# A mixture-of-experts stage with 32-slot blocks in four column groups instead of 64-slot blocks in two

## The reference

```python
logits = (x @ router_w) + router_b
top_v, top_i = lax.top_k(logits, 4)            # 4 of 32 experts for each token
gates = jax.nn.softmax(top_v, axis=-1)
...
hdn = xblk @ w1[e] + b1[e]                     # 1024 -> 2048
g, up = hdn[:, :D_FF], hdn[:, D_FF:]
act = (clip(up, -7, 7) + 1.0) * (g * jax.nn.sigmoid(g * 1.702))      # g = minimum(g, 7)
y = act @ w2[e] + b2[e]                        # 1024 -> 1024
x = x + g2 * sum over the token's experts of gate * y
```

## Time and profile before

| | |
|---|---|
| median of 3 runs | 1650.99 us (1648.49 to 1652.93) |
| profiled execution, its time | 1649.28 us |
| profiled execution, its span (first to last instruction) | 1647.5 us |
| first W1 matmul of the expert loop | 648.89 us |
| TensorE busy | 1548.8 us (94%) |
| mean granted TensorE clock | 0.965 |

### The profile page before, as it was taken

How to read it: one execution, slowest core, us unless ns; L and a number is a source line. 1 busy time by engine, 2 the same in 40 slices (tenths; PEclk the granted TensorE clock), 3 DMA queues, 4 the chain that set the end, 5 groups by cost and what they waited for, 6 DMA issues and landing times.

```text
span 1647.5 us, 20298 instructions
## 1 busy us (share of the span) xinstructions
PE 1548.8 (94%) x8093; PEld 661.6 (40%) x8094; DVE 474.2 (29%) x791; ACT 318.8 (19%) x579; POOL 108.9 (7%) x111
## 2 busy tenths in 40 slices
PE   4989899978989898999999999999999999999996
PEld 4555555545544455333333333333333333333332
DVE  2141222147346254222222222222222222222224
ACT  1123332120231232111111111111111111111110
POOL 0000000120433250000000000000000000000000
PEclk8989998898998997999999999999999999999999
DMA  9462441341332650999999999999593999999993
GB/s 355 185 257 111 194 164 58 115 145 64 128 126 105 240 193 32 415 425 429 428 429 428 428 429 429 428 429 428 239 408 161 415 427 429 429 427 429 429 427 130
DMA packets 38583, 491.95 MB, mean 299 GB/s; under 512 B 4784, under 2 KB 4912, under 8 KB 9744
## 3 DMA queue, kind: packets, MB, share of 16 engines
q1 hardware_dynamic: 34144, 477.33, 70.1%
q0 software_dynamic: 4400, 14.06, 2.8%
HBM read 487.05 MB, written 4.33 MB: 298 GB/s over the span
## 4 chain that ended last, share of the span: by engine, by line
PE 89%; DVE 4%; DMA 3%; ACT 2%; issue 1%; POOL 1%; SPq 0%; DVEq 0%; POOLq 0%; ACTq 0%
PE ps L1609 28%; PE ps L1264 17%; PE ps L1638 15%; PE ps L1572 6%; PE ps L1558 6%; PE ps L1271 4%; PE ps L1200 4%; DMA ring<-in_w_dense 2%; PE ps L1223 1%; PE ps L1216 1%; PE ps L1614 1%; PE ps L1322 1%; PE ps L1342 1%; ACT ring L555 1%; PE ps L1520 1%
## 5 line engine op out<-in xcount | busy, mean ns | idle before, releaser
L1609 PE MATMUL ps<-ring,arena 128*64 128x512 f32 x2176 | 480.2, 594 | 2.9 <-issue 2.9
L1264 PE MATMUL ps<-ring,xT 128*128 128x512 f32 x672 | 306.2, 613 | 3.2 <-DMA ring<-in_w_dense 2.4
L1609 PEld LDWEIGHTS ps<-ring,arena 128*64 128x64 f32 x2176 | 156.7, 137 | 308.2 <-issue 305.6
L1638 PE MATMUL ps<-ring,arena 128*64 128x512 f32 x1088 | 248.5, 598 | 0.0
L1178 DVE TENSOR_TENSOR U<-ps,U 128x1024 f32<-128x1024 f32 (+1 forms) x102 | 124.4, 1220 | 248.9 <-PE ps L1572 248.9
L1264 PEld LDWEIGHTS ps<-ring,xT 128*128 128x128 f32 x672 | 129.2, 196 | 162.6 <-issue 158.2
L1638 PEld LDWEIGHTS ps<-ring,arena 128*64 128x64 f32 x1088 | 72.1, 136 | 168.1 <-issue 142.3
L1572 PE MATMUL ps<-arena 64*128 64x512 f32 x420 | 119.7, 636 | 0.8 <-ACT arena L741 0.8
L1558 PE MATMUL ps<-T,arena 128*64 128x512 f32 (+1 forms) x420 | 104.3, 615 | 1.2 <-DVE arena L1068 1.2
L714 ACT ACTIVATE W<-ps 128x512 f32<-128x512 f32 x35 | 20.9, 598 | 338.5 <-PE ps L1558 338.5
L1169 DVE TENSOR_SCALAR arena<-ps 128x512 f32<-128x512 f32 x34 | 23.5, 692 | 217.5 <-PE ps L1614 217.5
(11 more groups left out here) (261 smaller groups left out, 1043.7 us busy)
## 6 DMA issues: line engine op xcount, KB each, us to landing
ring<-in_w_moe SPq DMA_DIRECT2D x192, 2048.0 KB, 14.5
ring<-in_w_dense SPq DMA_DIRECT2D x33, 2048.0 KB, 8.6
V<-in_state POOLq DMA_DIRECT2D x6, 256.0 KB, 8.2
out_sample_retention<-V POOLq DMA_DIRECT2D x6, 256.0 KB, 2.8
R<-in_x_prompt SPq DMA_DIRECT2D x1, 1024.0 KB, 17.1
arena<-in_cache_kT POOLq DMA_DIRECT2D x8, 128.0 KB, 3.5
arena<-in_cache_v POOLq DMA_DIRECT2D x8, 128.0 KB, 3.6
arena<-in_b_gate POOLq DMA_DIRECT2D x4, 256.0 KB, 4.4
```

The source lines that it names most:

```text
L1264: last = mm(banks[t][0], xT[:, k, t * P:t * P + P], wv[:, k, :], start=(k == 0), stop=(k == KD - 1))
L1609: last = mm(ps[64 * a:64 * a + 64, half, :], xgT[:, k, j % 2, :], wv[:, k, HALF * a:HALF * a + HALF], start=(j % 2 == 0 and k == 0), stop= ...
L1638: last = mm(ps[64 * a:64 * a + 64, 2, :], actT[:, k, j - 4, :], wv[:, k, HALF * a:HALF * a + HALF], start=(j == 4 and k == 0), stop=(j == ...
```

## The change

- `BLOCK` is 32. With the counts above 8 experts need one block (0, 2, 5, 7, 25, 26, 29, 31), 22 two, and experts 17 and 19 three: 58 blocks.
- The stationary operand has 32 columns, and the output columns are split in four groups `a` = 0 to 3, each on 32 columns of the array: 512 streamed columns for W1 (256 of `g` and 256 of `up`, one bank for both), 256 for W2, `gather` and `scatter`. The weights are laid out on the host to fit; a unit of W1 now holds a quarter of the input rows for `g` and `up` alike.
- The block's order on TensorE: W1 units 2 and 3, bias, scatter of both prompt tiles, transposes of the gates, then W1 units 0 and 1 of the next block (they wait for `xg_ready`), transposes of `h_act`, `gather` for the block after the next, W2 unit 4, `turn`, scatter of the sample tile, W2 unit 5. The last block's part stands behind the loop.
- TensorE and DVE read two entries of `table_i` in each round instead of one.
- `unit_used` becomes three counters, `used01`, `used23`, `used45`; SP waits for them.
- ACT's round begins with a wait for `used23` and `take_turned`, the copy into `xgT`, before the gelu.
- After the loop GpSimd (POOL) does the multiplication and addition of `U` for the two prompt tiles, DVE the others.

The core of the diff (the loops removed are printed above):

```diff
-BLOCK = 64
-MAX_BLOCKS = 64
+BLOCK = 32
+MAX_BLOCKS = 72
+QUARTER = 256
+GROUPS = D // QUARTER
...
+    xgT = cut(1536, 2, GROUPS, BLOCK)
+    actT = cut(1792, 2, GROUPS, BLOCK)
...
+    HID, OUT, XROWS, GATES, SCAT = 0, 1, 2, 3, 4
...
-                sp.wait_ge(unit_used, EXPERT_UNITS * before + j)
+                sp.wait_ge((used01, used23, used45)[j // 2], 2 * before + j % 2)
...
+        pool.wait_ge(table_ready, 1)
+        n_blocks = pool.value_load(table_i[0:1, MAX_BLOCKS:MAX_BLOCKS + 1], min_val=NEXP, max_val=MAX_BLOCKS - 1)
+        for t in range(2):
+            pool.wait_ge(added, 3 * n_blocks + t + 1)
+            nc.gpsimd.tensor_tensor(U[:, t, :], U[:, t, :], V[:, 0, :], ALU.mult).then_inc(pool_scaled, 1)
+            pool.wait_ge(pool_scaled, t + 1)
+            nc.gpsimd.tensor_tensor(R[:, t, :], R[:, t, :], U[:, t, :], ALU.add).then_inc(pool_summed, 1)
...
+        def gate_hidden(i):
+            act.wait_ge(g_cut_ready, i)
+            A(g_act, g_cut, ACT.Gelu_apprx_sigmoid).then_inc(g_act_ready, 1)
+            act.wait_ge(actT_done, i)
+            A(actT, ps[:, OUT, 0:QUARTER].rearrange("p (c a s) -> p c a s", c=2, a=GROUPS), ACT.Copy).then_inc(actT_ready, 1)
+        def take_gates_and_out(i):
+            act.wait_ge(gateT_done, i + 1)
+            act.wait_ge(scattered, 2 * i + 1)
+            A(gateT[:, 0:TOKENS], ps[:, GATES, 0:TOKENS], ACT.Copy).then_inc(gateT_ready, 1)
+            act.wait_ge(used45, 2 * i + 1)
+            A(y_blk, ps[:, OUT, 0:QUARTER], ACT.Copy).then_inc(y_ready, 1)
...
-        with act.Fori(1, n_blocks + 1) as i:
...
+        with act.Fori(1, n_blocks) as i:
+            act.wait_ge(used23, 2 * i + 1)
             take_turned(i + 1)
-            act.wait_ge(unit_used, EXPERT_UNITS * i + 5)
-            A(y_blk, ps[:, 2, :], ACT.Copy).then_inc(y_ready, 1)
+            gate_hidden(i)
+            take_gathered(i + 2)
+            take_gates_and_out(i)
+        gate_hidden(n_blocks)
+        take_gates_and_out(n_blocks)
...
+        def cut_hidden(i):
+            dve.wait_ge(used23, 2 * i + 1)
+            X.tensor_scalar(g_cut, ps[:, HID, 0:QUARTER], LIMIT, None, ALU.min).then_inc(g_cut_ready, 1)
+            X.tensor_scalar(u_cut, ps[:, HID, QUARTER:2 * QUARTER], LIMIT, -LIMIT, ALU.min, ALU.max).then_inc(u_cut_ready, 1)
+        def gate_hidden(i):
+            dve.wait_ge(u_cut_ready, i)
+            dve.wait_ge(g_act_ready, i)
+            X.scalar_tensor_tensor(out=h_act, in0=u_cut, scalar=1.0, in1=g_act, op0=ALU.add, op1=ALU.mult).then_inc(act_ready, 1)
...
-        with dve.Fori(1, n_blocks + 1) as i:
-            dve.wait_ge(picked, i)
-            dve.wait_ge(unit_used, EXPERT_UNITS * i - 1)
-            X.tensor_tensor(pick_gate, pick.unsqueeze(2).to_broadcast([P, 3, 2, BLOCK]),
-                            sel_now[:, 1, :].unsqueeze(2).unsqueeze(3).to_broadcast([P, 3, 2, BLOCK]), ALU.mult).then_inc(gates_picked, 1)
+        with dve.Fori(1, n_blocks) as i:
             e_next = dve.value_load(table_i[0:1, bass.ds(i, 1)], min_val=0, max_val=NEXP - 1)
-            dve.wait_ge(gates_picked, i)
...
+            e_after = dve.value_load(table_i[0:1, bass.ds(i + 1, 1)], min_val=0, max_val=NEXP - 1)
+            cut_hidden(i)
             pick_expert(e_next)
-            dve.wait_ge(dve_step, i + counts["dve_step"])
...
+            gate_hidden(i)
+            weigh_picks(i + 1)
+            dve.wait_ge(gathered, i + 1)
+            pick_tokens(i + 1, e_after, 2 * i + 2)
+            add_scattered(i)
+        cut_hidden(n_blocks)
+        gate_hidden(n_blocks)
+        add_scattered(n_blocks)
...
+        def scatter_tile(t, first, at):
+            r = ROWS[t]
+            for a in range(GROUPS):
+                last = mm(ps[0:r, first + a, at:at + QUARTER], gateT[32 * a:32 * a + 32, t * P:t * P + r], y_blk[32 * a:32 * a + 32, :], start=True, stop=True)
+            return last
...
+        def hidden(js, e):
+            for j in js:
+                unit_here(j, e)
+                wv = ring[:, j, :].rearrange("p (k a c) -> p k a c", k=2, a=GROUPS)
+                for k in range(2):
+                    c, b = divmod(2 * j + k, GROUPS)
+                    for a in range(GROUPS):
+                        last = mm(ps[32 * a:32 * a + 32, HID, :], xgT[:, c, b, :], wv[:, k, a, :],
+                                  start=(j == 0 and k == 0), stop=False, skip_group_check=True)
+                if j < 2:
+                    last.then_inc(used01, 1)
+                if j == 2:
+                    last.then_inc(used23, 1)
+        def hidden_bias(i):
+            pe.wait_ge(expert_picked, i)
+            for a in range(GROUPS):
+                last = mm(ps[32 * a:32 * a + 32, HID, :], pick_e[0:96], b1_by_group[0:96, :, a, :],
+                          start=False, stop=True, skip_group_check=True)
+            last.then_inc(used23, 1)
...
+        def output(j, e):
+            unit_here(j, e)
+            wv = ring[:, j, :].rearrange("p (k c) -> p k c", k=GROUPS)
+            for b in range(GROUPS):
+                for a in range(GROUPS):
+                    last = mm(ps[32 * a:32 * a + 32, OUT, 0:QUARTER], actT[:, j - 4, b, :], wv[:, b, QUARTER * a:QUARTER * a + QUARTER],
+                              start=(j == 4 and b == 0), stop=(j == 5 and b == 3), skip_group_check=True)
+            last.then_inc(used45, 1)
...
+        hidden((0, 1), 0)
+        gather(2)
+        turn(2)
+        with pe.Fori(1, n_blocks) as i:
             e = pe.value_load(table_i[0:1, bass.ds(i - 1, 1)], min_val=0, max_val=NEXP - 1)
-            pe.wait_ge(xg_ready, i)
...
+            e_next = pe.value_load(table_i[0:1, bass.ds(i, 1)], min_val=0, max_val=NEXP - 1)
+            hidden((2, 3), e)
+            hidden_bias(i)
+            scatter_prompt(i)
+            turn_gates(i)
+            pe.wait_ge(xg_ready, i + 1)
+            pe.wait_ge(g_cut_ready, i)
+            pe.wait_ge(u_cut_ready, i)
+            hidden((0, 1), e_next)
+            turn_hidden(i)
+            gather(i + 2)
             pe.wait_ge(actT_ready, i)
-            for j in (4, 5):
...
+            output(4, e)
+            turn(i + 2)
+            scatter_sample(i)
+            output(5, e)
+        hidden((2, 3), NEXP - 1)
+        hidden_bias(n_blocks)
+        scatter_prompt(n_blocks)
+        turn_gates(n_blocks)
+        turn_hidden(n_blocks)
+        pe.wait_ge(actT_ready, n_blocks)
+        output(4, NEXP - 1)
+        scatter_sample(n_blocks)
+        output(5, NEXP - 1)
+        scatter_prompt(n_blocks + 1)
+        scatter_tile(2, 0, 0).then_inc(scattered, 1)
...
-    w1 = x["moe_w1"][0].reshape(NEXP, 2, 4, P, 2, D).transpose(0, 4, 1, 3, 2, 5).reshape(NEXP, 4, P, 4 * D)
-    w2 = x["moe_w2"][0].reshape(NEXP, 2, 4, P, D).transpose(0, 1, 3, 2, 4).reshape(NEXP, 2, P, 4 * D)
+    w1 = x["moe_w1"][0].reshape(NEXP, 2, 2, 2, P, 2, GROUPS, QUARTER).transpose(0, 3, 1, 4, 2, 6, 5, 7).reshape(NEXP, 4, P, 4 * D)
+    w2 = x["moe_w2"][0].reshape(NEXP, GROUPS, 2, P, D).transpose(0, 2, 3, 1, 4).reshape(NEXP, 2, P, 4 * D)
```

More of the change, by code:

```diff
@@ L1152, in _, with add_scattered @@
+        def add_scattered(i):
+            for t, r in enumerate(ROWS):
+                dve.wait_ge(scattered, 2 * i if t < 2 else 2 * i + 1)
+                by_group = U[0:r, t, :].rearrange("p (a c) -> p a c", a=GROUPS)
+                at = QUARTER * (t % 2)
+                X.tensor_tensor(by_group, ps[0:r, SCAT:SCAT + GROUPS, at:at + QUARTER], by_group, ALU.add).then_inc(added, 1)
         pick_expert(0)
+        weigh_picks(1)
+        e_second = dve.value_load(table_i[0:1, 1:2], min_val=0, max_val=NEXP - 1)
@@ L1556, in gather @@
             for t, r in enumerate(ROWS):
-                for a in range(2):
-                    last = mm(ps[64 * a:64 * a + 64, 3, :], pick[0:r, t, :], T[0:r, t, HALF * a:HALF * a + HALF],
+                for a in range(GROUPS):
+                    last = mm(ps[32 * a:32 * a + 32, XROWS, 0:QUARTER], pick[0:r, t, :], T[0:r, t, QUARTER * a:QUARTER * a + QUARTER],
                               start=(t == 0), stop=(t == 2), skip_group_check=True)
@@ L1564, in turn @@
             pe.wait_ge(xg_rows, n)
-            for c in range(4):
-                last = tr(ps[:, 3, c * P:(c + 1) * P], xg_s[:, c * P:(c + 1) * P], P)
+            for c in range(2):
+                last = tr(ps[:, XROWS, c * P:(c + 1) * P], xg_s[:, c * P:(c + 1) * P], P)
             last.then_inc(turned, 1)
-        def scatter_tile(t, first):
-            for a in range(2):
-                last = mm(ps[:, first + a, :], gateT[64 * a:64 * a + 64, t * P:(t + 1) * P], y_blk[64 * a:64 * a + 64, :], start=True, stop=True)
-            last.then_inc(scattered, 1)
@@ new lines, in turn_gates, with turn_hidden @@
+        def turn_gates(i):
+            pe.wait_ge(gates_picked, i)
+            for t, r in enumerate(ROWS):
+                last = tr(ps[:, GATES, t * P:t * P + r], pick_gate[0:r, t, :, :], r)
+            last.then_inc(gateT_done, 1)
```

(13 more changed lines are left out.)

180 lines of the change are left out of this document (68 added, 112 removed).

## The result

The changed kernel takes 1710.35 us (median of 4, 1706.18 to 1713.65), the kernel before 1650.78 in the same session: ratio 1.036, 95% interval 1.0331 to 1.0388. The forecast was 1721, range 1670 to 1775. The profiled execution took 1713.65 us, with a span of 1711.8.

A forecast was written before the change was run, and what follows sets the result against it. TensorE alone was the loop's chain, with DMAs only just hidden. Terms 649.4 + 22.8 + 845.5 + 169.9 + 10.9 + 14.3 gave a 1712.8 us span, 1716 as median, plus 5 for clock: 1721 us, range 1670 to 1775.

The forecast's parts named there:

- What bounds: Expert loop before: TensorE alone is the chain, 28.84 us a block, DMAs only just hidden at 29.4 us an expert.
- P: Predicted length of one 32-slot block on TensorE, two waits included: 15.46 + 0.5 + 0.95 = 16.91 us.
- The rival near 1610 us: Expert loop: TensorE disappears behind the DMAs, 32 x 29.4 us and the ends, near 1610 us; chance 0.01.
- Streaming and shapes, 15.46 us: TensorE's block without waits: W1 7.33, scatter 1.69, gather 1.59, transposes 1.22, W2 3.63, together 15.46 us.
- the rival with 1786 us: Scatter: four row groups don't run at once, 12 steps, +1.29 us a block, 1786 us; chance 0.07.
- The table load ahead of the copy, 0.5 us: TensorE waits for `xg_ready` while ACT loads a table before copying: 0.5 us a block, between 0.3 and 0.6.
- the rival of 1831 us: ACT: a drain behind each table load delays `xg_ready` and the picks, +2.2 us, 1831 us; chance 0.03.
- The loop's head, 0.95 us: Round's start: branch and two register loads on TensorE's sequencer outlast the queued burst, 0.95 us a block, bounds 0.4 and 1.3.
- One-block experts, 28.1 us: Six middle experts, next W1 units 0 and 1 ahead of W2: 28.1 us each, one 29.4, together 169.9 us.
- the 5 us that I had for the clock: Lower clock after TensorE idles behind one-block experts: 1 us each for six or seven, 5 us added, bounds 0 and 15.
- The end, 14.3 us: From the last W2 matmul's end, with GpSimd's part on the path: 14.3 us against 16.1 before, gain 1.8.
- The rival with neither wait: Loop: sequencer and ACT run ahead as before, block 15.46 us, 1648 us or 1643 if the clock holds; chance 0.12.

## Why the prediction was right, step by step

- **What bounds.** Right: a two-block expert costs 2P, more than its 29.4 us of loading and than one block of 28.84. 22 such experts at 33.1 us are 94 us more than before; that is the loss. The six one-block experts in the middle add 11.5 more (184.5 against 6 x 28.84), since their loads set their length; the three-block experts, the first, the last and the end pay part of it back. The rival near 1610 us needed 2P below 29.4; it is 33.1, and 31.0 even with both waits gone.
- **Streaming and shapes, 15.46 us.** Measured 15.49 with both waits removed. Four column groups run together, and four row groups too (16 scatter records in 1.15 us, the sample tile 0.59 on the chain), so the rival with 1786 us is out. In pairs, 16 records would be 8 steps of 0.215, 1.7 us.
- **The table load ahead of the copy, 0.5 us.** The mechanism is right. Its size is 0.33, near the lower bound of 0.3: the transposes end 1.63 us behind the bias, not 1.54, and the wait and its register took less than 0.2. The next ACTIVATE follows the load by 0.01 us (1120.20 after 1118.91 + 1.28). The drain of about 1380 ns in the Trainium skill ("ScalarE: Activation LUTs", What ACT_TABLE_LOAD costs) isn't there, before or after, and with it the rival of 1831 us is out.
- **The loop's head, 0.95 us.** Mechanism right, size 0.72. The head takes 1.96 us (1129.52 to 1131.48) against 2.0 worked out. What was off is the queue: the branch is reached when 12 of the 32 matmuls have started, 1.46 us ahead of the burst's end, and I had 1.07 from 28 queued instructions. Some 36 are queued then (20 matmuls, 16 weight loads). Nor is that a fixed number: at 1116.01, in the W1 burst of the same loop, the sequencer stands 44 instructions ahead. So the 28 of the kernel before were no measure of what the queue holds, and what sets the lead at the branch is open. The Trainium skill's 64 ("TensorE: Matmul & The Clock Gate", Architectural detail) would put the branch at the burst's start, and leave next to no gap; no run here shows it. The register loads look like this:

```profile
L1710 PEldq TENSOR_LOAD <-table_i x1: 306/306/306, 1130.0 to 1130.0; - x1
...
L1711 PEldq TENSOR_LOAD <-table_i x1: 301/301/301, 1130.7 to 1130.7; - x1
```

- **One-block experts, 28.1 us.** This term was wrong: 30.8 on average, 14.6 us for the six. The larger part is a landing, told of below: unit 4 comes late, by 1.6, 2.5 and 2.0 us in experts 2, 5 and 7, 0.8 in expert 26 and 0.1 in experts 25 and 29, 7.1 in all. All that follows it in the queue shifts with it; for expert 5 the last unit lands 2.6 us later than worked out (823.40 against 820.8). The clock is 5.2: in three of the six the matmuls of the last unit take 3.64 instead of 1.92. That is the 5 us that I had for the clock, so its size was right. What is left, 2.3 us, is spread over the six. The last expert has the lateness too (2.4 us for its unit 4): W2 waits 2.02 and 0.76 us for units 4 and 5, which I had as landed, 14.7 instead of 10.9.
- **The end, 14.3 us.** 14.0.
- So P was 0.37 us too long (-18.6 us), one-block experts and the last too short (+14.6 and +3.8), and 1712.8 met a span of 1711.8 by errors that cancel. That closeness is luck; the two waits and the count of blocks are not. The 1721 came 11 us high by 1.0 of these, by the 5 for the clock (which the measured one-block experts already hold), and by the step from profile to median: I had added 1.7 us, but this profile is of the longest of the four runs, 3.3 above their median.
- **The rival with neither wait** had 1648 us. Made real it is 1.0047 of before, some 1658: its block was right, its one-block experts weren't. The side on which the change would be faster didn't exist, even then.

## What to carry over

Halving the tile of a loop that is bound by streaming pays only where it removes more passes than it adds: count the experts that fall on each side, and what the loads let the short ones keep. With the work between two waits halved, fixed costs that were hidden (a register load on the sequencer, a table load, a landing) come onto the path; look for them at the loop's head and behind every burst, and put them where the longest burst is still queued. When two engines are within a few per cent of each other, look whether what is saved on one comes back as waiting for the other. Here every profile of 58 shorter blocks has longer waits for the DMAs than the changed kernel's 69.6 us (71.7 to 90.0), but they don't follow the length of the block, and two profiles with equal blocks differ by 4 us; how much of a saving is lost that way isn't shown.

## What was not expected of the hardware

- **The clock falls behind short idling too.** With W1 behind W2, 2.53 and 0.75 us idle in each block brought the mean granted clock to 0.78 and 0.74 in the next two stretches of 3.5 us, and the gather from 1.64 to 2.26 us.
- **A unit issued shortly before another lands is late.** A load into an empty queue lands 7.4 us after its issue has ended; with four or more microseconds of transfers ahead of it, 4.9 after the one before. But unit 4 of expert 5, issued at 798.82 while the one ahead landed at 801.01, landed at 808.76, 7.7 behind that and 9.9 after its issue. In the changed kernel 37 loads are issued 1.5 to 3.5 us ahead of the previous landing, and they come on average 0.9 us later than both rules say, from not at all to 2.5 us. Which loads are hit changes from run to run: with the additions on DVE, which leave the loop as it is, unit 4 of the six one-block experts was late by 0.8 us in all instead of 7.1, only one of the six had its last unit at the lower clock, and they took 29.1 us each. The cause is open; no run was made for it.
- **DVE and GpSimd hold each other up** where both read two operands from SBUF: an addition of 1.22 us took 3.25, one of 2.35 took 3.21, as above. The rows look like taking turns, not like sharing: GpSimd's addition ends 2.2 us behind the end of DVE's L1225, and DVE's L1227 ends 1.1 us behind GpSimd's end. DVE's L1201, which reads one operand from PSUM (`ps`), ran at 1695.14 beside GpSimd's multiplication and took its usual 1.22, as another did at 1689.38. That the place of the operands decides it is an inference from these few rows.
